# Ending the first token tile of the down product three half slots early, and the second tile's column halves apart in the last layer

## The reference

```python
def _swiglu(x, w_gate, w_up, w_down):
    h = jax.nn.silu(jnp.einsum('bsd,df->bsf', x, w_gate)) * jnp.einsum('bsd,df->bsf', x, w_up)
    return jnp.einsum('bsf,fd->bsd', h, w_down)

def second_block(x, ...):
    for l in range(DEPTH_2):                       # DEPTH_2 = 2
        mix = _hybrid_mixer(x, rel_bias, w_in[l], ...)
        x = _layer_norm(ALPHA * x + mix, ln1_g[l], ln1_b[l])
        ffn = _swiglu(x, w_ffn_gate[l], w_ffn_up[l], w_ffn_down[l])
        x = _layer_norm(ALPHA * x + ffn, ln2_g[l], ln2_b[l])
    return x
```

## Time and profile before

| | before |
|---|---|
| median of 3 runs | 2426.46 us |
| lowest and highest | 2425.51 and 2428.31 us |
| the profiled execution | 2427.47 us |
| its span | 2425.6 us |
| granted TensorE clock, mean | 0.909 |
| PE busy | 2117.9 us (87%) |
| POOL busy | 1002.7 us (41%) |
| DVE busy | 778.8 us (32%) |
| ACT busy | 712.2 us (29%) |

### The profile page before, as it was taken

How to read it: one execution, slowest core, us unless ns; L and a number is a source line. 1 busy time by engine, 2 the same in 40 slices (tenths; PEclk the granted TensorE clock), 3 DMA queues, 4 the chain that set the end, 5 groups by cost and what they waited for, 6 DMA issues and landing times.

```text
span 2425.6 us, 31811 instructions
## 1 busy us (share of the span) xinstructions
PE 2117.9 (87%) x13380; PEld 1512.5 (62%) x13380; DVE 778.8 (32%) x1494; ACT 712.2 (29%) x852; POOL 1002.7 (41%) x324
## 2 busy tenths in 40 slices
PE   7999989677677667777668999999999999999998
PEld 3788974233233233333326887888887887888887
DVE  4566662111111111111112344533322253634331
ACT  1345520000000000000003545544543454644452
POOL 1356530000000000000006774887887774777886
PEclk9999997777878887787788999999999999999999
DMA  9485479999999999999997643565656743565653
GB/s 332 127 286 176 154 289 397 427 427 429 428 428 428 429 429 428 429 429 428 427 425 271 186 157 112 179 187 192 217 191 199 231 156 122 174 173 185 216 187 133
DMA packets 248672, 680.56 MB, mean 281 GB/s; under 512 B 8638, under 2 KB 173520, under 8 KB 222899
## 3 DMA queue, kind: packets, MB, share of 16 engines
q1 hardware_dynamic: 244672, 672.41, 73.5%
q10 hardware_dynamic: 3075, 4.65, 0.7%
q0 software_dynamic: 816, 1.94, 0.3%
HBM read 674.38 MB, written 4.59 MB: 280 GB/s over the span
## 4 chain that ended last, share of the span: by engine, by line
PE 65%; DMA 29%; DVE 3%; SPq 1%; issue 1%; ACT 0%; DVEq 0%; ACTq 0%
PE bank L2077 63%; DMA arena_sb<-w_exp 18%; DMA ring_sb<-w_exp 10%; PE bank L2080 2%; DMA ring_sb<-w_in 1%; SPq L678 1%; DVE arena_sb L1251 1%; DVE bank L1254 1%; DVE x_sb L1254 1%; DVE bank L1251 0%; DVE sm_sb L1824 0%; SPq L706 0%; DVE arena_parts L1251 0%; DVE sm_sb L1792 0%; ACT arena_parts L1131 0%
## 5 line engine op out<-in xcount | busy, mean ns | idle before, releaser
L827 POOL TENSOR_TENSOR ring_parts<-ring_sb,ring_parts 128x2048 fp32r<-128x2048 f32 x186 | 848.2, 4575 | 1222.6 <-ACT ring_parts L1083 1222.3
L2077 PE MATMUL bank<-arena_sb 128*32 128x512 f32 (+10 forms) x2862 | 390.2, 571 | 121.8 <-DMA arena_sb<-w_exp 107.0
L2077 PE MATMUL bank<-arena_parts,ring_parts 128*128 128x256 f32 (+1 forms) x2480 | 450.2, 330 | 2.2 <-issue 1.3
L2077 PE MATMUL bank<-hT_parts,ring_parts 128*128 128x256 f32 (+1 forms) x2208 | 430.5, 326 | 2.4 <-DVE arena_sb L1251 2.4
L2077 PEld LDWEIGHTS bank<-arena_parts,ring_parts 128*128 128x128 f32 x2480 | 382.4, 188 | 51.5 <-issue 2.1
L1083 ACT CAST ring_parts<-ring_sb 128x2048 fp32r<-128x2048 f32 x186 | 350.8, 1886 | 210.7 <-DMA ring_sb<-w_in 92.3
L2077 PE MATMUL bank<-ring_sb,arena_sb 128*32 128x512 f32 (+1 forms) x2240 | 265.2, 616 | 136.4 <-DMA ring_sb<-w_exp 133.9
L2077 PEld LDWEIGHTS bank<-hT_parts,ring_parts 128*128 128x128 f32 x2208 | 352.7, 189 | 41.8 <-issue 5.2
L1251 DVE TENSOR_TENSOR arena_sb<-bank,arena_sb 128x512 f32<-128x512 f32 (+4 forms) x239 | 137.9, 599 | 715.3 <-PE bank L2077 614.4
L2077 PEld LDWEIGHTS bank<-arena_sb 128*32 128x32 f32 (+5 forms) x2862 | 157.4, 150 | 316.7 <-DMA arena_sb<-w_exp 145.7
L2077 PE MATMUL bank<-ring_parts,arena_parts 128*128 128x512 f32 (+1 forms) x1248 | 284.6, 386 | 0.0
(11 more groups left out here) (266 smaller groups left out, 1315.3 us busy)
## 6 DMA issues: line engine op xcount, KB each, us to landing
ring_sb<-w_exp SPq DMA_DIRECT2D x96, 2048.0 KB, 35.5
arena_sb<-w_exp SPq DMA_DIRECT2D x93, 2048.0 KB, 35.9
ring_sb<-w_in SPq DMA_DIRECT2D x92, 1024.0 KB, 5.3
ring_sb<-w_ada SPq DMA_DIRECT2D x24, 1024.0 KB, 10.1
ring_sb<-w_ffn_gate SPq DMA_DIRECT2D x22, 1024.0 KB, 5.4
ring_sb<-w_ffn_up SPq DMA_DIRECT2D x22, 1024.0 KB, 5.3
ring_sb<-w_ffn_down SPq DMA_DIRECT2D x22, 1024.0 KB, 4.9
ring_sb<-w_in SPq DMA_DIRECT2D x42, 512.0 KB, 5.0
```

What stands on the lines that cost most here:

```text
L827: g.tensor_tensor(low, half(n)[0], high.bitcast(F32), ALU.subtract).then_inc(s["lo_ready"], 1)
L2077: return M.matmul(o, l, r, start=first, stop=last)
```

## The change

`late` goes from 9 to 8. So the products of half 8 on the second token tile are put behind all products of the first tile, as those of halves 9 and 10 already were. In the last layer the six late products run by columns: three for c = 0, then three for c = 1, where before each half's two stood together. In layer 0 they keep the order by halves, and the transposes stay ahead of the very last product.

```diff
-                late = NF // 2 - 2
+                late = NF // 2 - 3
                 for i in range(NF // 2):
 ...
                     for t in range(2 if i < late else 1):
                         for c in range(2):
                             down_product(i, t, c)
-                for i in range(late, NF // 2):
-                    for c in range(2):
-                        if i > late and c == 1 and l < DEPTH_2 - 1:
-                            turn_x(f"xT{l + 1}", 0, 8 * (l + 1))
-                        down_product(i, 1, c)
+                rest = [(i, c) for i in range(late, NF // 2) for c in range(2)]
+                if l == DEPTH_2 - 1:
+                    rest = [(i, c) for c in range(2) for i in range(late, NF // 2)]
+                for i, c in rest:
+                    if (i, c) == (NF // 2 - 1, 1) and l < DEPTH_2 - 1:
+                        turn_x(f"xT{l + 1}", 0, 8 * (l + 1))
+                    down_product(i, 1, c)
```

## The result

| | before | changed |
|---|---|---|
| median of 12 runs | 2425.46 us | 2429.45 us |
| lowest and highest | 2423.24 and 2428.31 us | 2427.98 and 2434.79 us |
| ratio, with its 95% interval | | 1.0018 (1.001 to 1.0026) |
| the profiled execution, and its span | 2427.47 and 2425.6 us | 2429.48 and 2427.7 us |

The changed kernel is 4.0 us slower by the medians, and by the interval of the ratio 2.4 to 6.3 us. The direction was forecast. The size forecast, 5.75 us, is larger than 4.0 but lies inside the interval.

A forecast was written before the change was run, and what follows sets the result against it. PE was taken as the bound in the two layers. Terms of +5.45 (held half), -0.2 (tail) and +0.5 (clock) summed to +5.75 us, giving a median of 2432.2 us, range 2429.8 to 2435.2.

The forecast's parts named there:

- What bounds the kernel: In the two layers PE is the bound; what holds it at the seam moves all of layer 1 and the end.
- Part 1: Half 10, both layers: PE waits some 1.1 us for POOL's low part; the first tile ends 1.6 us early.
- Part 2: Layer 0 seam: half 8 held longer, `va` 1 issued 6.5 us later, ACT's root behind its cast; +5.45 us.
- Part 3: Transposes at the seam, behind more products: a gain of some 0.3 us, unseen under the late root; term 0.
- Part 4: Tail: DVE starts 1.7 us early but waits for the last bank; -0.2 us, at most -1.2 without PE's POOL wait.
- Part 5: Behind PE's 4.6 us wait at the seam the clock falls to half rate; +0.5 us, 3 chances in 4.
- The sum: Whole kernel: +5.45 - 0.2 + 0.5 = +5.75 us, a median of 2432.2 us.
- rival C: Same mechanism, smaller: POOL's low part doesn't hold PE at half 10; +3.7 us, or 2430.2 us; chance 0.11.
- Rival D: Seam: ACT's root doesn't stand behind the late cast, so only product order counts; 2425.5 us; chance 0.08.
- rival B: Same mechanism, larger: slower landing (+1.3) or low clock costing its 2 us (+1.5); 2433.6 to 2436 us; chance 0.14.

The follow-up runs named there:

- the hold alone: Before's product order, but in layer 0 down half 8 is counted as used five products later; 571.06 us between the marks, ratio to before 1.0032.
- the root ahead of the cast: Changed kernel, but ACT takes the first tile's square root ahead of the cast of `va` 1; 566.79 us mark to mark, ratio to before 1.0008.
- The smallest hold: Before, with layer 0's second-tile products of half 8 put between the first tile's halves 9 and 10; 566.07 us mark to mark, ratio 1.0009.
- the wait filled: Before, with one second-tile product of half 8 between the first tile's halves 9 and 10 in the last layer; last bank at 21.76 us, ratio 1.0001.
- kept busy: Changed kernel plus 18 discarded matmuls ahead of layer 0's transposes, filling PE's wait; 569.70 us mark to mark, ratio to before 1.002.
- layer 0 alone: Changed order in layer 0 only, the last layer as before; 570.09 us mark to mark, ratio to before 1.003.
- four late: Changed kernel's layer 0 with four half slots late instead of three, last layer as before; 574.95 us mark to mark, ratio to before 1.0041.

## Why the prediction was right in kind and too large in size

**What bounds the kernel**: right. What the seam lost went through layer 1: 4.98 us at the reciprocal, 5.36 at the second mark.

**Part 1, PE's wait for POOL**: it is there in both layers, 0.76 and 0.78 us in the trace. I had said 1.1, but the moments are right: PE went on 11.61 us behind the mark (11.66 said) and DVE got the first bank at 13.27 (13.33 said). The sum counted the wait from where the next product would have started, 0.31 us ahead of the end of the one before; the trace counts it from that (modelled) end.

**Part 2, the held half**: right, and shown by two independent edits, the hold alone (sufficient) and the root ahead of the cast (ACT's order is the link). The load came 6.48 us later, where 6.5 was said. The term was 5.45 and measured 4.98. From the issue to the start of the cast it was 5.02 us (1844.82 to 1849.84), not 5.29, and ACT's root starts 1.80 us behind the start of the cast, not 1.94. Both are the term's own small rows; no step was missing. With all holds the reciprocal follows the load: 13.61, 17.36 and 21.51 us give 21.01, 24.58 and 28.84. The smallest hold costs less than its length, 1.4 for 2.7 us, because before the root had some 1.1 us to spare: it started at 1848.73, a reciprocal follows a waited-for root by 0.40 us (1851.64 to 1852.04), and DVE began it only at 1850.24, behind its scaling. The sum for the change has this slack in it, though the prediction says beside it that no slack could be seen.

**Part 3, the transposes**: nothing of the gain was seen, as said. With the root first PE does find the tokens ready (eight transposes in 1.03 us without a gap), but there the late cast holds the seam at its next place.

**Part 4, the tail**: -0.2 was said, and it is -0.15 at the last bank and about -0.1 at the end of the span. The wait for the low part is what kept it small: with the wait filled the same place gives the 1.2 us that the prediction named as the most.

**Part 5, the clock**: it fell, as given 3 chances in 4. +0.5 was said, and it is +0.6 at the input product and about +0.3 at the second mark. The rule of the Trainium skill (TensorE: Matmul & The Clock Gate, Part 1: The HAM clock gate), that an idle array falls to the half rate, agrees with the window at 0.50 and with the kernel that was kept busy at 1.00. Of the shorter waits some left the clock where it was and one didn't (below).

**The sum**: 5.75 was said; 5.28 is measured from the first mark, and 4.0 by the medians. The first difference is part 2's. The second I can't ascribe: the interval, 2.4 to 6.3 us, holds both, two kernels that lose as much in the trace are 6.4 us (layer 0 alone) and 4.5 us (kept busy) over before by their medians, and in the profiled executions the first mark alone lies between 1825.17 and 1830.64 us, among kernels that are the same up to there. The change by the ratio, 0.18%, lies just inside the 0.2% that I called no change and gave 0.18; the 0.80 for slower by more than that was too sure, with the forecast only 0.9 us beyond the bound. The range, 2429.8 to 2435.2 us, was counted from a median of 2426.46 for before, so it means 3.3 to 8.7 us more; twelve runs put before at 2425.46, and the 4.0 us stand near the range's lower end. By the medians that is rival C's number (3.7), by the traces the forecast's. The traces decide for the forecast's mechanism, not the time. Rival D (no root behind the cast) is excluded, rival C in its reason (POOL does hold PE), and rival B in its size.

## What to carry to other kernels

Before a use of a loaded tile is moved later, look up which load waits for its place, and then who stands behind that load's first consumer in program order: here a cast that nobody needed yet stood ahead of a square root on which the whole seam hung. Two events that end together in a trace, like the cast and the variance here, can hide a dependence: ask of each what it would hold if it came later. And a wait that a reordering opens can sometimes be filled with one of the moved pieces itself: in the last layer that gave 1.19 us in the trace. In layer 0 the same filling still cost 1.58, since it held the half.

## What was not expected

The clock fell behind a PE wait of 2.42 us (four late), while it stayed at 1.00 behind one of 2.10 (root first) and those of 0.76 and 0.78 us. The runs don't show what divides the 2.42 from the 2.10.

What the low level costs also differs from wait to wait. Of the 0.6 us that the changed kernel loses at the input product, 0.38 is left at the second mark; of 1.2 us in the hold alone, 1.05. In the hold alone the low level reaches into the input product itself, whose first twelve matmuls take 3.53 us there and 2.89 in the changed kernel. That PE's small waits behind the seam cover the rest is my reading; no run tests it.
